# Late modulation parts: transposed partial sums reduced by VectorE, in place of products with a column of ones

## The reference

```
mod = silu(c) @ w_ada + b_ada            # 1024 -> 6 x 1024
shift1, scale1, gate1, shift2, scale2, gate2 = split(mod, 6)
h = rmsnorm(x) * (1 + scale1) + shift1
z = h @ w_in                              # two branches: RG-LRU and spatial gating
x = x + gate1 * (merged @ w_out)
h = rmsnorm(x) * (1 + scale2) + shift2
x = x + gate2 * ((gelu(a) * b) @ w_down)  # a, b: conv(h @ w_up)
out = rmsnorm(x)
```

## Time and profile before

| | |
|---|---|
| median of 3 runs | 1518.69 us (1518.04 to 1519.09) |
| span of the profiled execution | 1517.1 us |
| median less span | 1.6 us |
| TensorE products | 1498.5 us busy, 99% |
| VectorE | 1250.8 us busy, 82% |
| ScalarE | 821.4 us busy, 54% |
| GpSimd | 414.0 us busy, 27% |

### The profile page before, as it was taken

How to read it: one execution, slowest core, us unless ns; L and a number is a source line. 1 busy time by engine, 2 the same in 40 slices (tenths; PEclk the granted TensorE clock), 3 DMA queues, 4 the chain that set the end, 5 groups by cost and what they waited for, 6 DMA issues and landing times.

```text
span 1517.1 us, 19716 instructions
## 1 busy us (share of the span) xinstructions
PE 1498.5 (99%) x6770; PEld 1234.8 (81%) x6770; DVE 1250.8 (82%) x1577; ACT 821.4 (54%) x1222; POOL 414.0 (27%) x307
## 2 busy tenths in 40 slices
PE   7999999999999999999999999999999999999998
PEld 4888888888888888888888788888888888888887
DVE  7997888777777786698859999999999987777775
ACT  5378888734454463423446456555555553444447
POOL 0123434523213323000100433333333321333324
PEclk9999999999999999999999999999999999999999
DMA  9532233374443364573421254444444436777722
GB/s 348 186 109 62 67 91 94 116 258 129 160 149 114 102 215 146 174 231 94 167 70 35 63 165 155 153 153 153 153 153 153 153 111 232 250 250 250 250 67 112
DMA packets 212227, 231.12 MB, mean 152 GB/s; under 512 B 9920, under 2 KB 164896, under 8 KB 211360
## 3 DMA queue, kind: packets, MB, share of 16 engines
q1 hardware_dynamic: 212128, 229.86, 45.8%
HBM read 167.95 MB, written 61.87 MB: 151 GB/s over the span
## 4 chain that ended last, share of the span: by engine, by line
PE 92%; DVE 6%; ACT 1%; issue 1%; DMA 0%; DVEq 0%; ACTq 0%
PE ps L886 74%; PE ps L964 4%; PE ps L985 3%; PE ps L1263 1%; PE ps L1110 1%; PE ps L1245 1%; PE ps L1027 1%; PE ps L1167 1%; PE ps L1071 1%; DVE wop L1914 1%; DVE hidw L2616 1%; DVE hq L2559 1%; PE ps L814 1%; DVE n L2551 0%; PE ps L1064 0%
## 5 line engine op out<-in xcount | busy, mean ns | idle before, releaser
L1326 ACT ACTIVATE wop<-raw 128x512 fp32r<-128x512 f32 (+1 forms) x541 | 307.2, 571 | 363.6 <-PE ps L886 240.2
L1914 DVE TENSOR_TENSOR wop<-raw,wop 128x512 fp32r<-128x512 f32 (+1 forms) x541 | 376.4, 699 | 120.1 <-ACT wop L1326 118.5
L727 POOL TENSOR_TENSOR raw<-raw,raw 128x512 f32<-128x512 f32 (+1 forms) x69 | 102.4, 1484 | 868.5 <-DVE wop L1914 423.2
L886 PE MATMUL ps<-hq,wop 128*128 128x512 f32 x888 | 213.9, 390 | 1.1 <-DVE wop L1914 0.9
L886 PEld LDWEIGHTS ps<-hq,wop 128*128 128x128 f32 x888 | 166.3, 188 | 37.6 <-DVE wop L1914 1.3
L886 PE MATMUL ps<-dq,wop 128*128 128x512 f32 x840 | 190.6, 389 | 0.0
L886 PE MATMUL ps<-yq,wop 128*128 128x512 f32 x792 | 190.3, 389 | 0.0
L886 PEld LDWEIGHTS ps<-dq,wop 128*128 128x128 f32 x840 | 157.7, 188 | 32.7
L886 PEld LDWEIGHTS ps<-yq,wop 128*128 128x128 f32 x792 | 148.6, 188 | 30.9
L1928 DVE TENSOR_TENSOR ps<-ps,snap_p 128x512 f32<-128x512 f32 x136 | 94.5, 695 | 48.9 <-PE ps L886 48.3
L1341 ACT ACTIVATE snap_p<-ps 128x512 f32<-128x512 f32 x136 | 81.2, 597 | 98.9 <-PE ps L886 98.8
(11 more groups left out here) (290 smaller groups left out, 2582.2 us busy)
## 6 DMA issues: line engine op xcount, KB each, us to landing
dq<-hid_keep SPq DMA_DIRECT2D x35, 1024.0 KB, 7.3
raw<-in_w_in SPq DMA_DIRECT2D x96, 256.0 KB, 4.1
raw<-in_w_up SPq DMA_DIRECT2D x96, 256.0 KB, 3.3
hid_keep<-part_b SPq DMA_DIRECT2D x40, 512.0 KB, 3.0
hid_keep<-part_t SPq DMA_DIRECT2D x20, 512.0 KB, 3.1
raw<-in_w_down SPq DMA_DIRECT2D x80, 128.0 KB, 2.3
ada_w<-in_w_ada SPq DMA_DIRECT2D x8, 1024.0 KB, 11.4
gate_keep<-tg SPq DMA_DIRECT2D x16, 512.0 KB, 4.5
```

The lines of the kernel that those rows point to most:

```text
L727: nc.gpsimd.tensor_tensor(s1, a21, a22, ALU.add).then_inc(s_made, 1)
L886: done = nc.tensor.matmul(bank, left[:, w, lk, :], right[:, x, rk, :], start=(first and w == 0 and x == 0), stop=(last and w == 1), skip_g ...
L1326: nc.scalar.activation(wop[n % 4][:, 0, 0:depth[n], :], raw[slot][:, 0:depth[n], :], ACT.Copy).then_inc(f_hi, 1)
L1914: V.tensor_tensor(wop[n % 4][:, 1, 0:kd, :], raw[slot_of[n][0]][:, 0:kd, :], wop[n % 4][:, 0, 0:kd, :].bitcast(F32), ALU.subtract).then_in ...
```

## The change

A new function turned transposes each block of 128 columns of the partial sum on TensorE, with the identity, so that the 128 partial values of a channel come to lie along the free dimension of one partition. VectorE then reduces along the free dimension into mod and adds b_ada in a second instruction, which waits for the first. Both uses are changed, the eight quarters (two blocks each) and the two whole parts (eight blocks each). The early vectors still use column_sums.

```
+            def turned(acc, n, bank):
+                for j in range(n):
+                    last = nc.tensor.transpose(blocks(bank)[:, j, :], acc[:, j * P:(j + 1) * P], ident[:, :])
+                return last
...
-                        column_sums(quarter_acc, QC // P, past[1][:, 0, 0:QC // P]).then_inc(ada_psum, 1)
+                        turned(quarter_acc, QC // P, past[1]).then_inc(ada_psum, 1)
...
-                        column_sums(ada_acc, KT, BANKS[(pos - 1) % 2][0][:, 0, 0:KT]).then_inc(ada_psum, 1)
+                        turned(ada_acc, KT, BANKS[(pos - 1) % 2][0]).then_inc(ada_psum, 1)
...
             def quarter_columns(j, bank):
                 n, c0 = QC // P, 2 * KT + QC // P * j
                 dve.wait_ge(ada_psum, j + 1)
-                V.tensor_tensor(mod[:, c0:c0 + n], bank[:, 0, 0:n], C("b_ada", c0, n), ALU.add).then_inc(mod_ready, 1)
+                step(V.tensor_reduce(mod[:, c0:c0 + n], blocks(bank)[:, 0:n, :], axis=AX, op=ALU.add))
+                V.tensor_tensor(mod[:, c0:c0 + n], mod[:, c0:c0 + n], C("b_ada", c0, n), ALU.add).then_inc(mod_ready, 1)
...
             def mod_part(e, bank):
                 dve.wait_ge(ada_psum, QUARTERS + e - 1)
-                V.tensor_tensor(mod[:, (e + 2) * KT:(e + 3) * KT], bank[:, 0, 0:KT], C("b_ada", (e + 2) * KT, KT), ALU.add)\
-                 .then_inc(mod_ready, 1)
+                part = mod[:, (e + 2) * KT:(e + 3) * KT]
+                step(V.tensor_reduce(part, blocks(bank), axis=AX, op=ALU.add))
+                V.tensor_tensor(part, part, C("b_ada", (e + 2) * KT, KT), ALU.add).then_inc(mod_ready, 1)
```

## The result

The changed kernel takes 1524.97 us (median of 5 runs, 1524.56 to 1525.6); beside it on the same chip the kernel before took 1518.82 (5 runs, 1518.04 to 1519.28). The ratio is 1.0042, with a 95% interval of 1.0031 to 1.0053. It is slower by 6.1 us, where 3.2 us less was forecast, and the time lies above the range. The profiled execution has a span of 1523.9 us, 6.8 more than the 1517.1 of before.

A forecast was written before the change was run, and what follows sets the result against it. TensorE was taken to bound the kernel (busy 99% of the span). Savings of 1.05 (seven blocks), 0.26 (eighth quarter), 0.94 (B1) and 0.94 (B3) sum to 3.2 us: 1518.69 - 3.2 = 1515.5 us, range 1514.2 to 1518.1.

The forecast's parts named there:

- What VectorE takes on: VectorE's column adds: a reduction in front of each, 0.42 us a quarter and 1.22 a whole part, delays 0.46 and 1.26.
- the mixing wait of step 4 grows: Rival, blocks 1 to 7: costs 7 x (delay - 0.61), slower from a delay of 0.91 us; chance 0.06.
- TensorE's own saving: All ten places: transposes for products with ones save 0.26 us a quarter and 0.94 a whole part, 3.96 in all.
- The reductions: VectorE, quarters and whole parts: 0.42 us for 256 elements and 1.22 for 1024, taken from the PSUM copy row.
- The scan-like case: Rival, all reductions: as dear as the scan, delays 0.73 and 2.33 us, only 0.5 saved, 1518.2; chance 0.12.
- The slack of seven blocks: Blocks 1 to 7, vhat before the mixing products: slack 0.61 us against a delay of 0.46, 0.15 gained a block, 1.05 together.
- The eighth quarter: Unit ZU2, where no v_norm follows: the full 0.26 us is saved.
- The wait ahead of A0: TensorE's one wait, 0.3 us at 567: hangs on a chain TensorE itself releases, so it moves up with everything.
- B1: First whole part: VectorE held 1.26 us longer, 1.03 of idle at 673.19 takes that up; full 0.94 saved.
- O0: Behind the second whole part (B3): gate_b(6) 0.46 us late against 0.88 of slack, third sum not delayed; full 0.94 saved.
- late in the last branch: Rival: gate_b(6)'s 0.46 us reaches O0's third sum, or the string to A0 doesn't move whole; 2.2 saved, 1516.5; chance 0.14.
- No change after 730: Sign to look for in the new trace: no change before 340 us and after 730.

The follow-up runs named there:

- Run 1: Changed kernel, but the quarter's reduction writes back to PSUM and the add reads it there; 1519.26 us against 1518.76 for the kernel before.
- run 2: Changed kernel, but GpSimd's first weight sum of each unit behind a quarter waits until the add is done; 1518.78 us, ratio 1.0000.
- run 5: Kernel before, with two small copies ahead of the quarters' add so it reads SBUF, no transposes or reductions; 1525.01 us against 1518.74.
- run 7: Changed kernel with quarters' transposes behind the mixing products, reductions later, bias added once for all four parts in O0; 1517.14 us against 1518.74.
- run 3: Changed kernel with only the two whole parts transposed and reduced, quarters as in the kernel before; 1518.48 us, ratio 1.0000.
- run 10: The kernel of run 7 measured once more, unchanged; 1516.66 us, ratio 0.9986 to the kernel before.
- run 8: The kernel of run 7 with products of ones again in the two whole parts; 1518.52 us, ratio 0.9997 to the kernel before.
- run 6: Changed kernel with TensorE's two waits ahead of the mixing products swapped, vhat's now last; 1524.48 us, ratio 1.0034 to the kernel before.

## Why the prediction was wrong

**The step that failed** is in "What VectorE takes on": "Each add from a few PSUM columns (0.15 us, row of L2151 in the earlier trace rows) gets a reduction in front". The add was kept at 0.15 us although the change does two things to it: it moves its first input from PSUM to SBUF, and by the reduction it moves the add from just ahead of GpSimd's weight sum (0.01 us in six blocks) to inside it. It takes 1.02 us, because an add from two SBUF inputs doesn't end before the sum under way does. Run 1 takes away the one condition and run 2 the other, and run 5 shows that nothing else of the change is needed. Whether an add from SBUF at its old place, just ahead of the sum, would have been short, no run shows.

By its own sum, with the measured sizes: the delay of vhat is 0.46 + 0.87 = 1.33 us and not 0.46. Its slack was put at 0.61, of which 0.06 + 0.11 were allowed for the release. The release takes 0.17 more than that 0.06 (0.23 measured, since vhat's wait is an instruction by itself with a second wait behind it; the row at 863 had one wait alone), so the slack is 0.44. 1.33 − 0.44 = 0.89 us more a block, measured 0.91. In place of 1.05 gained in the seven blocks, 6.5 is lost. Of this difference of 7.5 the add makes 7 x 0.87 = 6.1 and the release 7 x 0.17 = 1.2. The prediction's own formula for the slower rival, 7 x (delay − 0.61), gives 5.0 at this delay, and with the slack mended 6.2; the traces show 6.5 up to block 7. So the rival "the mixing wait of step 4 grows" is what happened, at its place and beyond its point of decision (a delay of 0.91), and it had been given 0.06. It asked only for a slower reduction, and so found "beyond any row" what another instruction supplied.

**Could it have been seen?** Yes, in rows of the kernel before that weren't read. VectorE has another instruction with two SBUF tensors, the quarter's pieces of L2145. Without a GpSimd sum beside it, and beside one (timeline of before):

```profile
340.79 0.48 DVE L2145 SCALAR_TENSOR_TENSOR quarter_ring<-quarter_ring,cact,quarter_ring 128x256 f32<-128x256 f32 x1 [0.56 <-DMA quarter_ring<-in_w_ada]
```

```profile
346.18 1.67 POOL L730 TENSOR_TENSOR raw<-raw,raw 128x512 f32<-128x512 f32 x1
...
346.63 1.50 DVE L2145 SCALAR_TENSOR_TENSOR quarter_ring<-quarter_ring,cact,quarter_ring 128x256 f32<-128x256 f32 x1
```

One form, 0.48 and 1.50 us. Over the whole trace of before, those that start during a GpSimd sum take 1.48 us on average (9 of them), the others 0.48 (39); the low parts of 128x512 (L1914) 1.27 (76) and 0.68 (325). Instructions of the same size with a PSUM input show no such difference: the sums of L1928 from ps and snap_p take 0.696 (80) and 0.693 us (56). And the timeline was read without GpSimd, so the sum that starts just behind the add didn't show. It starts 0.40 us behind it in that block and 0.01 in the other six, both within the 0.46 by which the add was to move.

The Trainium skill says it outright: "SBUF — State Buffer", section "SBUF: two separate sides", has VectorE and GpSimd share a pair of ports under an exclusive lock; a VectorE operation with two SBUF inputs and a GpSimd operation that reads SBUF block each other for the whole instruction, whichever starts first. Runs 1, 2 and 5 agree, for a sum that starts first: the held adds end 0.02 us behind the end of the sum, each time. An estimate by that page's rule, with this trace's durations, is a delay of up to 1.30 + 0.46 in seven blocks, so up to 7 x (1.76 − 0.61) = 8 us lost there and, less the 2.1 gained elsewhere, up to 5.9 us slower; 6.1 was measured.

**The other steps, in order.**
- TensorE's own saving: right. In the B units 1.89 against 1.88. A quarter gives 0.29 a block in run 7 (0.26 forecast, 0.29 its top).
- The reductions: right, 0.419 and 1.218 (0.42 and 1.22). The scan-like case is out: the reduction of 1024 took what the copy of 1024 takes in the earlier trace rows. The base rate that the Trainium skill names ("VectorE: DVE Perf Modes", "Rules for kernel authors") held; that this operation would be the slowest of its engine did not, beside the scan's 2.29.
- The slack of seven blocks: 0.61 forecast, 0.44 found. Run 1 shows this term by itself, since its add is short: 0.46 − 0.44 is a loss of 0.02 a block, measured 0.05, where the forecast's 0.15 of gain was expected. Even with a short add, the change as placed brings nothing in the blocks.
- The eighth quarter: its add is short, 0.16, as GpSimd is idle there.
- The wait ahead of A0: it was to move up with everything. In the changed kernel it grew from 0.3 to 0.6 us. In the other profiles TensorE's place there shifts against before by anything from 0.6 sooner to 0.9 later, so this stretch isn't steady between executions; the cause is open.
- B1: full saving in its units, as forecast. But the idle of 1.03 at 673.19 did not absorb the reduction as claimed: VectorE's idle there hangs on a transfer that itself starts later by the reduction (0.74 of it is left).
- O0: ahead of the third sum the weight load sat idle for 0.78 us where it was 0.21 in the earlier trace rows, and 0.55 of the saving is gone between its first product and its third sum. The rival "late in the last branch" is borne out in this profile; its cause isn't shown, since runs 3 and 10, with the same whole parts, lose nothing there.
- A sum in a rival: the scan-like case has B3 at 0.1; by its own figures it is 0.94 − (1.53 − 0.88) = 0.29. Nothing else hangs on it.
- "No change after 730": wrong for the profiled execution, which loses 0.6 at the hidden units and 1.3 behind the last transposes. The other kernels' profiles show between 0 and 1.1 and between 0 and 1.5 there, with no relation to what was changed in them. The spread of the runs is wider too, 2.7 to 3.8 us in runs 1, 2, 3 and 8, against 1.7 to 2.1 of before beside them. The cause is open; a single profile tells nothing below 1.5 us of these stretches.

## What to carry to other kernels

When an edit moves an operand of a VectorE instruction from PSUM to SBUF, look up what GpSimd does at that moment: an add of two columns that took 0.15 us took 1.02 beside a GpSimd sum, and the rows that show this are other two-input instructions of the same trace, sorted by whether GpSimd was busy when they started. Look also at the sum that starts just behind the instruction, when the edit makes it later. Tiny instructions in front of a critical one deserve this look most. And if a small result isn't needed for long (here the modulation columns, first used in O0), take its steps out of the tight string altogether rather than make them cheaper in place: that turned 6.1 us slower into 1.6 to 2.1 us faster (runs 7 and 10).

## What the hardware showed that was not expected

- An add of 128x2 from two SBUF inputs is held by a GpSimd tensor add of 128x512 until this ends: 1.02 to 1.18 us instead of 0.16. A reduction or an add that reads PSUM isn't held beside the same kind of sum (0.42 and 0.16).
- From the end of a VectorE instruction to TensorE's next weight load it took 0.06 us where the load itself carries the wait (863 us), 0.07 in block 0 of the change, where one instruction that only waits stands between and had been waiting for 4 us, 0.12 in run 6 with one such instruction, and 0.23 in blocks 1 to 7 of the change with two.
- 32 transposes of 128x128 in ten groups in place of 32 products with one column left the granted clock at 1.00 in the blocks and in the B units.
